# State-space recurrence taken in steps of two, and one half gate tile in four split by VectorE

## The chip, the cores and the metric

The kernel runs on one core of a Trainium2 chip. The metric is the device time of one execution in microseconds, lower is better. Engines: TensorE (PE in the profile, its weight loads PEld), VectorE (DVE), ScalarE (ACT), GpSimd (POOL), SyncE (SP).

## What is computed

An encoder block on 256 tokens of width 2048 with 16 meta tokens put ahead (272 positions): a projection `h @ w_in` gives the state-space inputs, queries, keys, values and 32 tiles of gates. A bidirectional state-space mixer and a windowed attention run in parallel, are gated, merged and projected, and a product-key expert network follows. The part that the change rewrites:

```python
a = exp(lam * dt)                        # complex, per group and state
bu = einsum('lgc,gpc->lgp', u, Bbar)     # 16 channels -> 64 states
h[l] = a * h[l-1] + bu[l]                # forward, and once more backward
y = real(einsum('lgp,gcp->lgc', h, C))
y = gelu(y_fwd + y_bwd + d_skip * u)
...
gates = h_norm @ w_in[:, gates] + b_gate # 32 tiles of 128 columns
```

## The kernel before

Products that want fp32 precision are made from a high part (`float32r`) and a low part of each operand, three matmuls in place of one: high by high, high by low, low by high.

The stage that the change touches runs two loops in step with each other, in 32 steps and a few to drain. **The gate tiles**: gate tile n (16 blocks of 128 by 128 weights, contracted with 256 tokens) comes in two halves, h = 2n and 2n+1; half h lies in slot q = h mod 4 of `halves`, the high part in `gate_hi(q)`, the low in `gate_lo(q)`. For every half GpSimd's queue issues two transfers. `cast_half(h)` (L385) loads the weights into `gate_hi` with the cast to `float32r`. ScalarE writes the negative of it into `gate_lo` (`minus_high`, L523), and `rest_half(h)` (L389) loads the same weights again and adds them there, so that weights minus high part remain. The order on the queue is cast(h+1), rest(h), cast(h+2), rest(h+1), and each waits in line: an even cast for the first half of the tile before it to be used by TensorE (`s_gh`), an odd cast for tile h//2 - 2 to be finished (`s_wdone`), a rest for its `minus_high`. TensorE multiplies the half in `half_gate` (L1269 to L1271, 24 matmuls of 256 columns), two steps behind (`LAG`).

**The recurrence**: in step t (four steps to a column tile of 128 channels, `cc`) the four engines handle two groups of states in one direction. ScalarE makes turning angles, sines and cosines over 272 positions (L516, L517, L541 to L544). TensorE projects the inputs to states (`state_inputs`, L1312, 12 matmuls into four banks of `ps`). VectorE turns them back by the angle (L910, L911, L916, L917), so that the complex recurrence becomes two real ones, scans them (L926, four scans of 272), turns forward again (L937, L938) and takes real parts (L945). TensorE multiplies by the output matrices (`state_outputs`, L1326), which ScalarE and VectorE build (L533, L890, L891). VectorE adds the direct term (`take_y`, L952).

The order of the work is written out by hand. VectorE's step t begins with the products of tile t-2 (L910), then real parts of t-3, the scans, the angles and L937, L938. TensorE's step t is: first half of gate tile t-2, `state_inputs` of t-1, which waits for VectorE's products of t-2 because both use the same banks, `state_outputs` of t-3, second half of gate tile t-2. Every engine takes its instructions in order.

Of the kernel before, what the change touches and what calls it, by code (L numbers as in the profile page):

```python
# [56 lines left out]
NSC = 6  # L57


def build(nc, W, keys, par, bw, cw, meta, x, gffn, gfin, u_tab, v_tab, out):  # L60
    top = ExitStack()
    with top:
# [48 lines left out]
        scur = sbt(mix, "scur", [P, 2, NSC, SPC])  # L111
# [10 lines left out]
        bwH = sbt(scan, "bwH", [P, 2, 2, 2, P], F32R)  # L122
        cp = sbt(scan, "cp", [P, 2, 2, SPC, 32])
        cs = sbt(scan, "cs", [P, 4, SPC, 32])
        tb = sbt(scan, "tb", [P, 2, 2, L])
        ang = sbt(scan, "ang", [P, 2, 2, L])
        trig = sbt(scan, "trig", [P, 2, 2, 2, L])
        pa = sbt(scan, "pa", [P, 2, 2, L])
        pb = sbt(scan, "pb", [P, 2, 2, L])
# [3 lines left out]
        gated = sbt(post, "gated", [P, 2, 2, SEQ])  # L133
# [7 lines left out]
        def in_hs2(at):  # L141
            return h2f[:, at * D:(at + 1) * D].rearrange("p (s u r t) -> p s u r t", s=2, u=2, r=2)
        oc, os_ = in_hs2(0), in_hs2(1)

# [93 lines left out]
        s_cp = sem("s_cp")  # L238
        s_bu = sem("s_bu")
# [13 lines left out]
        s_gh = sem("s_gh")  # L253
        s_gel, s_sgg, s_glu, s_sig, s_ya = sem("s_gel"), sem("s_sgg"), sem("s_glu"), sem("s_sig"), sem("s_ya")
# [43 lines left out]

        def gate_hi(q):
            return halves[:, q, :]  # L300

        def gate_lo(q):
            return halves[:, 4 + q, :]

# [10 lines left out]
        def _(sp):  # L315
# [15 lines left out]
            with sp.Fori(0, CT // 2) as b:  # L331
                for cc in range(2):
                    sp.wait_ge(s_bu, PPC * (2 * b + cc) + PPC)
                    sp.dma_start(bwt[:, cc, :, :, :].rearrange("p d r s -> p (d r s)"),
                                 bw[bass.ds(2 * b + cc, 1), :, :].rearrange("a p n -> (a p) n")).then_inc(s_bw[cc], 16)
                    sp.wait_ge(s_cp, 2 * (2 * b + cc) + 2)
                    sp.dma_start(cwt[:, cc, :, :, :].rearrange("p i r c -> p (i r c)"),
                                 cw[bass.ds(2 * b + cc, 1), :, :].rearrange("a p n -> (a p) n")).then_inc(s_cw[cc], 16)
# [21 lines left out]
        def _(pool):  # L360
# [63 lines left out]
        def _(act):  # L424
# [81 lines left out]
            def turns(b, t):  # L506
# [7 lines left out]
                for u in range(2):  # L514
                    turn = scur[:, cc, 0, at + 2 * u:at + 2 * u + 1]
                    nc.scalar.activation(tb[:, t % 2, u, :], iota, ACT.Copy, scale=turn)  # L516
                    ins = nc.scalar.activation(ang[:, t % 2, u, :], iota, ACT.Identity, scale=turn, bias=magic[:, :])  # L517
                ins.then_inc(s_tb, 1)

            def minus_high(b, t, half):  # L520
                use, q = gate_half(b, t, half)
                act.wait_ge(s_gc[q], 16 * use + 16)
                nc.scalar.activation(gate_lo(q), gate_hi(q), ACT.Copy, scale=-1.0).then_inc(s_gn, 1)  # L523

            def out_products(b, cc, k):

                ct = 2 * b + cc
                if k == 0:
                    act.wait_ge(s_cw[cc], 16 * b + 16)
                    act.wait_ge(s_cp, 2 * ct + 4)  # L530
                c, co = ((0, 2), (1, 3), (0, 4), (1, 2))[k]
                for i in range(SPC):
                    ins = nc.scalar.activation(cs[:, k, i, :], cwt[:, cc, i, c, :], ACT.Copy, scale=scur[:, cc, co, i:i + 1])  # L533
                ins.then_inc(s_cpl, 1)
# [19 lines left out]
            def inputs_high(b, cc):  # L554
                nc.scalar.activation(uP[:, cc, 0, :], ucur[:, cc, :], ACT.Copy).then_inc(s_inH, 1)
                act.wait_ge(s_bw[cc], 16 * b + 16)
                nc.scalar.activation(bwH[:, cc, :, :, :].rearrange("p d r s -> p (d r s)"),
                                     bwt[:, cc, :, :, :].rearrange("p d r s -> p (d r s)"), ACT.Copy).then_inc(s_inH, 1)

            def scan_body(b, first=False):  # L560
                for t in range(PPL):
                    turns(b, t)
# [7 lines left out]
                    if t % PPC < 2:  # L570
                        for k in range(2):
                            out_products(b, t // PPC, 2 * (t % PPC) + k)
                    if t >= LAG + 1 or not first:
                        gate(*behind(b, t, LAG + 1))

            scan_body(0, first=True)
            with act.Fori(1, BODIES) as b:
                scan_body(b)
            minus_high(*behind(BODIES, 0, 1), 0)
# [4 lines left out]

            act.wait_ge(s_ye, 2 + CT)
# [119 lines left out]
        def _(dve):  # L705
            dve.sem_inc(s_cp, 4)
# [27 lines left out]
            def discretise():  # L734
# [48 lines left out]
                for k, a in enumerate((4, 10, 16, 18, 19)):  # L783
# [85 lines left out]
            def scalars(b, cc):  # L869
# [4 lines left out]
                                      scal[:, bass.ds(ct, 1), :, :].rearrange("p a k i -> p (a k i)")).then_inc(s_scur, 1)  # L874
                nc.vector.tensor_copy(ucur[:, cc, :], flat(ukT[:, bass.ds(ct, 1), :])).then_inc(s_scur, 1)
                dve.wait_ge(s_scur, 2 * ct + 2)

            def inputs_low(b, cc):
                dve.wait_ge(s_inH, 2 * (2 * b + cc) + 2)
                nc.vector.tensor_tensor(uP[:, cc, 1, :], ucur[:, cc, :], uP[:, cc, 0, :], ALU.subtract).then_inc(s_inL, 1)  # L880
                nc.vector.tensor_tensor(bwL[:, cc, :, :, :].rearrange("p d r s -> p (d r s)"),
                                        bwt[:, cc, :, :, :].rearrange("p d r s -> p (d r s)"),
                                        bwH[:, cc, :, :, :].rearrange("p d r s -> p (d r s)"), ALU.subtract).then_inc(s_inL, 1)

            def out_matrices(b, cc):

                ct = 2 * b + cc
                dve.wait_ge(s_cpl, 4 * ct + 4)
                dve.wait_ge(s_y, PPC * ct + PPC)
                nc.vector.tensor_tensor(cp[:, cc, 0], cs[:, 0], cs[:, 1], ALU.subtract).then_inc(s_cp, 1)  # L890
                nc.vector.tensor_tensor(cp[:, cc, 1], cs[:, 2], cs[:, 3], ALU.subtract).then_inc(s_cp, 1)  # L891
# [9 lines left out]
            def input_products(b, t):  # L901
# [4 lines left out]
                bu = ps[:, 2:6, 0:L].rearrange("p (u r) t -> p u r t", u=2)  # L906

                def turn(k):
                    return trig[:, s, k, :, :].rearrange("p u (o t) -> p u o t", o=1).broadcast_to([P, 2, 2, L])
# [9 lines left out]
            def scans(b, t):  # L919
                n, cc = PPL * b + t, t // PPC  # L920
                at = units(t).start
                for k in range(2):
                    dve.wait_ge(s_gin, 2 * n + 1 + k)
                    for u in range(2):
                        r = scur[:, cc, 1, at + 2 * u:at + 2 * u + 1].broadcast_to([P, L])
# [3 lines left out]
            def turned_back(b, t):  # L929

                s, n, kept = t % 2, PPL * b + t, slice(0, SEQ) if t % 2 else slice(META, L)
# [3 lines left out]
                def turn(k):  # L935
                    return trig[:, s, k, :, kept].rearrange("p u (o t) -> p u o t", o=1).broadcast_to([P, 2, 2, SEQ])
                nc.vector.tensor_tensor(oc[:, s], turn(0), pa[:, :, :, kept], ALU.mult).then_inc(s_oc, 1)  # L937
                nc.vector.tensor_tensor(os_[:, s], turn(1), pa[:, :, :, kept], ALU.mult).then_inc(s_os, 1)  # L938
# [9 lines left out]
            def take_y(b, cc):  # L948

                ct = 2 * b + cc  # L950
                dve.wait_ge(s_y, PPC * ct + PPC + PPL)
                nc.vector.scalar_tensor_tensor(flat(yT[:, bass.ds(ct, 1), :]), ucur[:, cc, META:L],  # L952
                                               scur[:, cc, 5, 0:1], ps[:, 6 + cc, 0:SEQ], ALU.mult, ALU.add
                                               ).then_inc(s_ye, 1)
# [11 lines left out]
            def scan_body(b, first=False):  # L966
                for t in range(PPL):
                    if t % PPC == 0:
                        scalars(b, t // PPC)
                        if first and t == 0:  # L970
                            angles(b, t)
                            inputs_low(b, 0)
                    pair(b, t, first)
                    if t == PPL - 1:
                        take_y(b, 0)
                    if t == PPC - 1 and not first:
                        take_y(b - 1, 1)
# [4 lines left out]
                    if t % PPC == 0 and not (first and t == 0):  # L982
                        inputs_low(b, t // PPC)
                    if t % PPC == 2:
                        out_matrices(b, t // PPC)

            scan_body(0, first=True)
            with dve.Fori(1, BODIES) as b:
                scan_body(b)
            for t in range(2):  # L990
                pair(BODIES, t)
                turned_back(*behind(BODIES, t, 2))
            real_parts(*behind(BODIES, 2, 3))
            take_y(BODIES - 1, 1)


# [153 lines left out]
        def _(pe):  # L1150
# [4 lines left out]
            pe.sem_inc(s_gh, 2)  # L1155

# [104 lines left out]
            def half_gate(b, t, half):  # L1261
# [3 lines left out]
                pe.wait_ge(s_ga[q], 16 * use + 16)  # L1265
# [31 lines left out]

            def state_inputs(b, t):
                n = PPL * b + t
                cc, way, jp = place(t)  # L1300
                if t % PPC == 0:
                    pe.wait_ge(s_inL, 2 * (2 * b + cc) + 2)
                pe.wait_ge(s_ab, 2 * n + 2)
                for r in range(2):
                    for part in range(3):
                        for u in range(2):
                            rows = slice(32 * (2 * jp + u), 32 * (2 * jp + u) + 32)
                            w = (bwL if part == 2 else bwH)[rows, cc, way, r, :]
                            x = uP[rows, cc, part % 2, :]
                            if way:  # L1310
                                x = x[:, L - 1::-1]
# [251 lines left out]
```

## Time and profile before

| | us |
|---|---|
| median of 3 runs (lowest, highest) | 2129.09 (2126.37, 2129.18) |
| profiled execution, its own time | 2125.94 |
| its span | 2124.1 |

| engine | busy us | share of the span |
|---|---|---|
| TensorE matmuls | 1744.0 | 82% |
| VectorE | 1381.1 | 65% |
| ScalarE | 549.3 | 26% |
| GpSimd | 804.1 | 38% |

The span falls into stages: projections and attention to about 205 us, the stage described above from there to 549 us (its last result is the GELU on `yT`), gating, merge and output projection to about 770 us, then the experts to the end. In the stage of the change GpSimd's instructions are few and short: most of its time is waiting. Times are microseconds, and those marked ns are nanoseconds.

### The profile page before, as it was taken

The numbers are of one execution on the slowest core, as the hardware profiler recorded it, in microseconds if no ns is written. First come the engines' busy times: TensorE is split into PE (matmuls) and PEld (weight loads), VectorE is DVE, ScalarE is ACT, GpSimd is POOL, SyncE is SP. The second block draws the span as 40 slices with busy tenths as digits, with TensorE's granted clock in tenths as the row PEclk, the third lists the DMA queues.
The fourth block names the chain that finished last, engine by engine and source line by source line (L and its number), as shares of the span: only waits on it lengthen the run. The fifth ranks groups of instructions, "written<-read, shape, count | busy, mean of one in ns | idle before, by whom it ended". The sixth has DMA issues, their size and how long they took to land.

```text
span 2124.1 us, 23420 instructions
## 1 busy us (share of the span) xinstructions
PE 1744.0 (82%) x7552; PEld 1078.5 (51%) x7552; DVE 1381.1 (65%) x2230; ACT 549.3 (26%) x1167; POOL 804.1 (38%) x686
## 2 busy tenths in 40 slices
PE   7987788888899998978977997777877777777776
PEld 6976677777799885524533543222322222222222
DVE  5444999999545446566565666666666666666654
ACT  5333877777434321010110110001001001000001
POOL 1041222222054014453544454543545654644431
PEclk9998899999999999999999999999999999999999
DMA  4430899999655569999999999999999999999997
GB/s 193 159 120 21 207 213 220 218 213 217 212 178 183 180 227 423 421 421 409 423 420 395 400 404 422 421 421 422 406 422 421 422 422 422 422 422 421 421 421 299
DMA packets 106665, 694.82 MB, mean 327 GB/s; under 512 B 11856, under 2 KB 11856, under 8 KB 30928
## 3 DMA queue, kind: packets, MB, share of 16 engines
q0 software_dynamic: 92160, 604.02, 74.9%
q1 hardware_dynamic: 14432, 89.90, 11.5%
q8 instruction: 36, 0.59, 0.1%
q14 instruction: 37, 0.30, 0.0%
HBM read 691.78 MB, written 2.10 MB: 327 GB/s over the span
## 4 chain that ended last, share of the span: by engine, by line
PE 37%; DMA 36%; DVE 10%; issue 9%; ACT 4%; POOL 3%; DVEq 0%; POOLq 0%; ACTq 0%; SPq 0%
DMA uv<-u_tab,eid 30%; PE ps L1466 14%; DMA halves<-W 6%; PE ps L1172 3%; PE ps L1416 3%; PE ps L1174 3%; PE ps L1173 3%; POOL uv L420 2%; DVE uv L1111 2%; PE ps L1399 1%; PE ps L1400 1%; PE ps L1398 1%; PE ps L1165 1%; ACT cs L533 1%; POOL uv L417 1%
## 5 line engine op out<-in xcount | busy, mean ns | idle before, releaser
L1466 PE MATMUL ps<-uv,dg 128*128 128x512 f32 x2048 | 953.7, 611 | 273.2 <-DVE dg L1117 267.8
L1111 DVE CUSTOM_DVE_ANT_0 uv<-uv,xn 128x2048 f32<-128x2048 f32 x256 | 587.1, 2293 | 378.2 <-DMA uv<-u_tab,eid 359.6
L1466 PEld LDWEIGHTS ps<-uv,dg 128*128 128x128 f32 x2048 | 378.2, 193 | 826.1 <-issue 462.2
L420 POOL DMA_INDIRECT uv<-v_tab,eid x256 | 273.1, 1067 | 601.8 <-PE ps L1466 347.8
L417 POOL DMA_INDIRECT uv<-u_tab,eid x256 | 344.5, 1346 | 199.8 <-issue 186.1
L678 ACT ACTIVATE ga<-av 128x1 f32<-128x1 f32 x256 | 51.9, 203 | 1180.9 <-DVE av L1111 1180.9
L1269 PE MATMUL ps<-hH,halves 128*128 128x256 f32 x512 | 154.4, 302 | 53.6 <-DMA halves<-W 31.7
L731 DVE TENSOR_TENSOR low_ring<-ring,wh 128x2048 fp32r<-128x2048 f32 x43 | 101.2, 2356 | 76.4 <-ACT wh L440 76.3
L1270 PE MATMUL ps<-hLx,halves 128*128 128x256 f32 x512 | 148.4, 290 | 0.0
L1271 PE MATMUL ps<-hH,halves 128*128 128x256 f32 x512 | 148.2, 289 | 0.0
L389 POOL DMA_DIRECT2D halves<-W x64 | 55.7, 870 | 222.6 <-ACT halves L523 222.6
L1269 PEld LDWEIGHTS ps<-hH,halves 128*128 128x128 f32 x512 | 101.3, 198 | 71.9 <-issue 34.1
L1117 DVE TENSOR_SCALAR dg<-prm,ga,gw 128x128 f32<-128x128 f32 x256 | 93.7, 366 | 67.6 <-ACT ga L678 32.3
L440 ACT ACTIVATE wh<-ring 128x2048 fp32r<-128x2048 f32 x52 | 99.5, 1914 | 137.3 <-PE ps L1174 98.1
L1270 PEld LDWEIGHTS ps<-hLx,halves 128*128 128x128 f32 x512 | 101.5, 198 | 0.0
L1271 PEld LDWEIGHTS ps<-hH,halves 128*128 128x128 f32 x512 | 101.3, 198 | 0.0
L1416 PE MATMUL ps<-h2T,ring 128*128 128x256 f32 x448 | 100.8, 379 | 0.0
L1416 PEld LDWEIGHTS ps<-h2T,ring 128*128 128x128 f32 x448 | 85.1, 190 | 21.7 <-issue 11.5
L1172 PE MATMUL ps<-hH,wh 128*128 128x272 f32 (+1 forms) x288 | 85.6, 297 | 2.0 <-DVE hL L816 1.1
L523 ACT ACTIVATE halves<-halves 128x1024 fp32r<-128x1024 f32 x64 | 67.6, 1056 | 68.8 <-DMA halves<-W 68.7
L1173 PE MATMUL ps<-hL,wh 128*128 128x272 f32 (+1 forms) x288 | 82.9, 288 | 0.0
L1174 PE MATMUL ps<-hH,low_ring 128*128 128x272 f32 (+1 forms) x288 | 82.8, 288 | 0.0
(247 smaller groups left out, 2359.4 us busy)
## 6 DMA issues: line engine op xcount, KB each, us to landing
ring<-W SPq DMA_DIRECT2D x72, 1024.0 KB, 4.8
halves<-W POOLq DMA_DIRECT2D x128, 512.0 KB, 6.8
xn<-x SPq DMA_DIRECT2D x4, 1024.0 KB, 9.8
uv<-u_tab,eid POOLq DMA_INDIRECT x256, 15.3
uv<-v_tab,eid POOLq DMA_INDIRECT x256, 14.0
bwt<-bw SPq DMA_DIRECT2D x8, 256.0 KB, 7.2
cwt<-cw SPq DMA_DIRECT2D x8, 256.0 KB, 7.2
out<-xn SPq DMA_DIRECT2D x4, 512.0 KB, 5.5
```

What stands on the lines that cost most here:

```text
L417: pool.indirect_dma_start(uv[:, s, 0, :], None, u_tab, at).then_inc(s_u[s], 16)
L420: pool.indirect_dma_start(uv[:, s, 1, :], None, v_tab, at).then_inc(s_vv[s], 16)
L731: nc.vector.tensor_tensor(low_ring[:, n % RING, :], ring[:, n % RING, :], high_slot(n), ALU.subtract).then_inc(s_low, 1)
L1111: nc.vector.tensor_tensor_reduce(uv[:, j % UV, 0, :], uv[:, j % UV, 0, :], xn[:, T, :], 1.0, 0.0, ALU.mult, ALU.add, av[:, hh, j:j + 1]).t ...
L1172: nc.tensor.matmul(dst, wh[:, block0 + k, :], xh(k), start=(k == 0), stop=False)
L1173: nc.tensor.matmul(dst, wh[:, block0 + k, :], xl(k), start=False, stop=False)
L1174: ins = nc.tensor.matmul(dst, wl[:, block0 + k, :], xh(k), start=False, stop=(k == last))
L1269: nc.tensor.matmul(ps[:, t % 2, 0:SEQ], wh[:, m, :], hH[:, k, META:L], start=(k == 0), stop=False)
L1270: nc.tensor.matmul(ps[:, t % 2, 0:SEQ], wh[:, m, :], hLx[:, k, :], start=False, stop=False)
L1271: ins = nc.tensor.matmul(ps[:, t % 2, 0:SEQ], wl[:, m, :], hH[:, k, META:L], start=False, stop=(k == KT - 1))
L1416: ins = nc.tensor.matmul(ps[:, 4 + q % 2, 0:SEQ], w[:, k, :], h2T[:, k, :], start=(k == 0), stop=(k == KT - 1))
L1466: ins = nc.tensor.matmul(ps[:, 4 * T + n, :], dg[:, j % 2, :], uv[:, j % UV, 1, n * 512:(n + 1) * 512], start=False, stop=last and i == 2 ...
```

## The change

The recurrence goes in steps of two: `h[l+1] = a*a*h[l-1] + (a*Bbar*u[l] + Bbar*u[l+1])`. The scan then runs over 136 elements, and so do angles, sines and turning products. The projection to states now takes even and odd positions with two sets of weights, `Bbar` and `a*Bbar`; the second is built per column tile by a transpose on TensorE (`input_turns`), a copy on ScalarE (`input_rows`), six VectorE products and sums (`stepped_inputs`) and a transpose back (`stepped_turns`). Outputs at the positions in between come from output matrices multiplied by `a`, so these have 64 columns, and from a direct term `kb` (TensorE `direct_terms`, 16 small matmuls for each column tile, and VectorE `direct_terms`), which also takes in `d_skip`. Output products move from ScalarE to VectorE, and `take_y` from VectorE to ScalarE. Ten small VectorE steps join the discretisation.

Of the gate halves, those with q = 3 (each second half of an odd tile) are loaded plainly into `plain`, a part of the weight ring free in this stage. VectorE subtracts the high part (`gate_rest`, once in every even step), for which it waits for both transfers; the plain load is queued where the accumulating one was, after `cast_half(h+1)`, and waits for nothing itself. `minus_high` is left out for these.

```diff
+        plain = ring[:, RING - 1, D // 2:D]
             def rest_half(h):
-                pool.wait_ge(s_gn, h + 1)
-                pool.dma_start(gate_lo(h % 4), half_weights(h), accum_op=ALU.add).then_inc(s_ga[h % 4], 16)
+                if h % 4 == 3:
+                    pool.dma_start(plain, half_weights(h)).then_inc(s_ga[3], 16)
+                else:
+                    pool.wait_ge(s_gn, 3 * (h // 4) + h % 4 + 1)
+                    pool.dma_start(gate_lo(h % 4), half_weights(h), accum_op=ALU.add).then_inc(s_ga[h % 4], 16)
...
+            def input_rows(b, cc):
+                act.wait_ge(s_bt, ct + 1)
+                act.wait_ge(s_kb, ct + 1)
+                nc.scalar.activation(bs[cc]..., ps[:, 4, :], ACT.Copy).then_inc(s_bs, 1)
+            def take_y(b, cc):
+                for j in range(4):
+                    for q in range(2):
+                        ins = nc.scalar.activation(..., ACT.Copy)
...
+            def stepped_inputs(b, cc):
+                nc.vector.tensor_copy(acur..., scal...).then_inc(s_acur, 1)
+                for k, (r, c) in enumerate(((0, 0), (1, 1), (1, 0), (0, 1))):
+                    nc.vector.tensor_tensor(am[:, k], bs[cc]..., four(acur[:, c, :]), ALU.mult).then_inc(s_am, 1)
+                for r, op in enumerate((ALU.subtract, ALU.add)):
+                    nc.vector.tensor_tensor(ab[:, :, r, :]..., am[:, 2 * r], am[:, 2 * r + 1], op).then_inc(s_abm, 1)
...
+            def out_products(b, cc, q):
+                for k, (c, of) in enumerate(((cre, kr), (cim, ki), (cre, kn), (cim, kr))):
+                    nc.vector.tensor_tensor(cs[:, k], c, co(of), ALU.mult).then_inc(s_cpl, 1)
...
+            def gate_rest(b, t):
+                use, q = gate_half(b, t, 1)
+                dve.wait_ge(s_gc[q], 16 * use + 16)
+                dve.wait_ge(s_ga[q], 16 * use + 16)
+                nc.vector.tensor_tensor(gate_lo(q), plain, gate_hi(q), ALU.subtract).then_inc(s_glo, 1)
...
                     pair(b, t, first)
                     if not (first and t == 0):
                         angles(b, t)
                     if t >= 2 or not first:
                         turned_back(*behind(b, t, 2))
+                    if t % 2 == 0 and (t or not first):
+                        gate_rest(*behind(b, t, 1))
+                    if t % PPC == 0:
+                        if not (first and t == 0):
+                            inputs_low(b, cc)
+                        out_products(b, cc, 0)
+                    elif t % PPC == 1:
+                        out_matrices(b, cc, 0)
+                        out_products(b, cc, 1)
+                    elif t % PPC == 2:
+                        out_matrices(b, cc, 1)
+                        if not (last and cc):
+                            stepped_inputs(*after(b, t))
+                    else:
+                        direct_terms(b, cc)
...
             def half_gate(b, t, half):
-                pe.wait_ge(s_ga[q], 16 * use + 16)
+                if q == 3:
+                    pe.wait_ge(s_glo, use + 1)
+                else:
+                    pe.wait_ge(s_ga[q], 16 * use + 16)
...
             def state_inputs(b, t):
                 for r in range(2):
+                    for odd in range(2):
+                        for part in range(3):
+                            for u in range(2):
+                                ins = nc.tensor.matmul(ps[:, 2 + u, r * H2:(r + 1) * H2], w, x, ...)
...
                     if t >= 1 or not first:
                         state_inputs(*behind(b, t, 1))
+                    if t % PPC == 1 and not (last and cc):
+                        input_turns(*after(b, t))
+                    if t % PPC == 3:
+                        direct_terms(b, cc, last and cc == 1)
+                        if not (last and cc):
+                            stepped_turns(*after(b, t))
                     if t >= 3 or not first:
                         state_outputs(*behind(b, t, 3))
```

## Rows read from the trace of the kernel before

**Rows 1.** Windows; window, length, busy by engine (instructions), granted clock, DMA share, GB/s.

```profile
291.00:332.00 41.00, 35.72 (x292) 30.47 (x290) 40.60 (x55) 30.73 (x71) 11.34 (x16) 0.96 0.96 223
```

**Rows 2.** Timeline of VectorE, one step; start, duration, line, operation, shapes.

```profile
329.88 0.43 DVE L880 TENSOR_TENSOR uP<-ucur,uP 128x272 fp32r<-128x272 f32 x1
330.24 0.68 DVE L881 TENSOR_TENSOR bwL<-bwt,bwH 128x512 fp32r<-128x512 f32 x1
330.84 1.28 DVE L910 TENSOR_TENSOR pa<-ps,trig 128x1088 f32<-128x1088 f32 x1
...
333.24 0.68 DVE L945 TENSOR_TENSOR hs<-hs 128x512 f32<-128x512 f32 x1
333.84 0.72 DVE L916 TENSOR_TENSOR pa<-pa,pb 128x544 f32<-128x544 f32 x1
...
335.11 2.56 DVE L926 TENSOR_TENSOR_SCAN pa<-scur,pa 128x272 f32<-128x272 f32 x4
337.59 0.70 DVE L898 SCALAR_TENSOR_TENSOR ang<-ang,tb 128x544 f32<-128x544 f32 x1
338.20 1.22 DVE L937 TENSOR_TENSOR hs<-trig,pa 128x1024 f32<-128x1024 f32 x1
339.34 1.22 DVE L938 TENSOR_TENSOR hs<-trig,pa 128x1024 f32<-128x1024 f32 x1
340.67 1.29 DVE L910 TENSOR_TENSOR pa<-ps,trig 128x1088 f32<-128x1088 f32 x1
```

**Rows 3.** Timeline, issues of half tiles and those who waited for their landing.

```profile
356.83 0.86 POOL L389 DMA_DIRECT2D halves<-W  x1 [3.27 <-ACT halves L523]
357.38 0.87 POOL L385 DMA_DIRECT2D halves<-W  x1
360.60 0.88 POOL L389 DMA_DIRECT2D halves<-W  x1 [2.35 <-ACT halves L523]
361.41 0.62 POOL L385 DMA_DIRECT2D halves<-W  x1
...
363.12 0.58 PE L1269 MATMUL ps<-hH,halves 128*128 128x256 f32 x1 [2.00 <-DMA halves<-W]
364.39 1.06 ACT L523 ACTIVATE halves<-halves 128x1024 fp32r<-128x1024 f32 x1 [0.84 <-DMA halves<-W]
...
367.47 0.28 PE L1271 MATMUL ps<-hH,halves 128*128 128x256 f32 x1
...
368.05 0.55 POOL L385 DMA_DIRECT2D halves<-W  x1 [1.43 <-PE ps L1271]
...
368.69 1.06 ACT L523 ACTIVATE halves<-halves 128x1024 fp32r<-128x1024 f32 x1 [0.67 <-DMA halves<-W]
```

**Rows 4.** From issue to landing, of the casting loads (L385, 64 of them).

```profile
DMA to landing us min/median/max: 3.9/7.0/9.0
```

**Rows 5.** From issue to landing, of the accumulating loads (L389, 64 of them).

```profile
DMA to landing us min/median/max: 5.2/6.8/9.3
```

**Rows 6.** Timeline of TensorE, inputs, outputs and a second half's start.

```profile
355.46 0.52 PE L1312 MATMUL ps<-uP,bwH 32*128 32x272 f32 x4
...
356.41 1.49 PE L1326 MATMUL ps<-hs,cp 128*32 128x256 f32 x12
...
358.02 0.39 PE L1269 MATMUL ps<-hH,halves 128*128 128x256 f32 x1
```

**Rows 7.** Windows around a wait of TensorE's; columns as in rows 1.

```profile
361.00:363.20 2.20, 0.20 (x2) 0.09 (x1) 1.85 (x5) 1.60 (x4) 1.03 (x2) 0.99 1.02 302
363.20:366.50 3.30, 3.30 (x16) 3.30 (x17) 3.30 (x5) 2.46 (x5) 0.76 (x1) 0.50 0.92 194
...
342.00:344.00 2.00, 0.00 (x0) 0.00 (x0) 2.00 (x3) 2.00 (x10) 0.55 (x1) 1.00 1.06 268
344.00:346.00 2.00, 1.82 (x15) 1.82 (x16) 2.00 (x4) 2.00 (x5) 0.00 (x0) 1.00 1.00 231
```

**Rows 8.** Lines of the attention stage: transposes on TensorE.

```profile
L1247 PE MATMUL ps<-prm,pr 128*128 128x128 f32 x32 | 6.9, 301 | 0.0
```

More of the change, by code:

```diff
@@ L569, in scan_body @@
                         minus_high(*behind(b, t, 1), 1)
-                    if t % PPC < 2:
-                        for k in range(2):
-                            out_products(b, t // PPC, 2 * (t % PPC) + k)
+                    if t % PPC == 2 and not (last and t > PPC):
+                        input_rows(*after(b, t))
                     if t >= LAG + 1 or not first:
                         gate(*behind(b, t, LAG + 1))
+                    if t == PPL - 1:
+                        take_y(b, 0)
+                    if t == PPC - 1 and not first:
+                        take_y(b - 1, 1)
             scan_body(0, first=True)
-            with act.Fori(1, BODIES) as b:
+            with act.Fori(1, BODIES - 1) as b:
                 scan_body(b)
+            scan_body(BODIES - 1, last=True)
             minus_high(*behind(BODIES, 0, 1), 0)
@@ L964, in pair, with scan_body @@
                     scans(*behind(b, t, 2))
[L966 removed]
+            def scan_body(b, first=False, last=False):
                 for t in range(PPL):
+                    cc = t // PPC
                     if t % PPC == 0:
[L969 removed]
+                        scalars(b, cc)
                         if first and t == 0:
+                            stepped_inputs(b, 0)
                             angles(b, t)
@@ L981, in scan_body @@
                         turned_back(*behind(b, t, 2))
[L982 to L985, printed above, removed]
+                    if t % 2 == 0 and (t or not first):
[13 more added lines that the diff above has]
+                        direct_terms(b, cc)
+            dve.wait_ge(s_wdone, RING + W_GATE)
+            for j in range(4):
+                nc.vector.tensor_copy(eye32[32 * j:32 * j + 32, :], ident[32 * j:32 * j + 32, 32 * j:32 * j + 32]).then_inc(s_eye, 1)
+            for a in (oc, os_):
+                nc.vector.memset(a[:, 1, :, :, 0:1], 0.0).then_inc(s_eye, 1)
+            dve.wait_ge(s_eye, 6)
             scan_body(0, first=True)
-            with dve.Fori(1, BODIES) as b:
+            with dve.Fori(1, BODIES - 1) as b:
                 scan_body(b)
+            scan_body(BODIES - 1, last=True)
             for t in range(2):
@@ L992, in _ @@
                 turned_back(*behind(BODIES, t, 2))
+                if t == 0:
+                    gate_rest(*behind(BODIES, t, 1))
             real_parts(*behind(BODIES, 2, 3))
-            take_y(BODIES - 1, 1)
             dve.wait_ge(s_ybh, 1)
```

251 lines of the change are left out of this document (184 added, 67 removed).

## The prediction

> **What bounds the kernel now.** I read the page's row of busy tenths first, to find the stage, then the windows, then the timeline of one step, then who waits for whom. In a window of 41 us GpSimd issues 16 transfers, which is four gate tiles, so a tile takes 10.25 us and two tiles 20.5 us [rows 1]. VectorE is busy for 40.6 of the 41 us: it is the bound. The DMA engines are at 0.96 beside it, TensorE's matmuls at 35.7 of 41 and ScalarE at 30.7. VectorE's step is 9.83 us from one L910 to the next [rows 2]; once in four steps extras come on top. The reader is to see two things in the rows: VectorE is full, and it waits for no transfer. Everything that a half gate tile needs passes over DMA, ScalarE, GpSimd's queue and TensorE, in a ring that VectorE is not part of.
>
> **What the change takes off.** From the spacing of starts, an operation of 272 elements takes 0.36 us, one of 512 takes 0.60, of 544 some 0.62 and of 1024 1.14 [rows 2]; on that line 256 elements are 0.34 and 128 are 0.22. The step has two products at 1.20, real parts at 0.60, two sums at 0.63, four scans at 0.62, the angles at 0.61 and two products at 1.14: 9.8. With halved lengths that is 2 x 0.62 + 0.35 + 2 x 0.36 + 4 x 0.35 + 0.36 + 2 x 0.60 = 5.3 us.
>
> Added on VectorE: `gate_rest`, 1024 elements, 1.14 in each even step. In a step t mod 4 = 0 `inputs_low` (0.36 + 2 x 0.60) and `out_products` (4 x 0.34), 2.9 in all; in t mod 4 = 2 four matrix parts of 128 (0.9) and `stepped_inputs` (six of 256, a small copy, two waits, 2.3), 3.2 in all; the mean after `gate_rest` is k = 3.05. Odd steps get 2.3 or 0.2, 1.2 in the mean. Two steps: 2 x 5.3 + 1.14 + 3.05 + 1.2 + 0.2 (scalars) = 16.2, or 8.1 a tile in place of 10.25. If VectorE's work were all, the stage would gain 69 us over 32 tiles.
>
> DMA: of four transfers in flight, the ones issued at 356.83 and 357.38 land at 363.1 and 364.35, and the cast issued at 361.41 at 368.65, behind one more accumulating load [rows 3]. So a cast takes 1.3 us of the queue and a pair 4.3, which leaves 3.0 for an accumulating load. Two tiles now use about 19.5 us (20.5 x 0.96 [rows 1]); one accumulating load turned into a plain one, taken at a cast's price, saves 1.7: 17.8. (A plain load isn't in these rows; the ends are nothing, were it as slow as an accumulating one, and a cast's 1.3 or a little less.)
>
> TensorE, over two tiles: four half tiles at 2.85 (24 x 0.118 [rows 6]); inputs 24 matmuls of 136 columns in place of 12 of 272, which took 0.95 [rows 6]: between 0.95, were it columns that count, and 1.9, were it instructions; each still loads weights of 128 columns, so I take 1.6. Outputs took 1.42 to 1.6 and halve to 0.8. New: in t mod 4 = 1 four transposes (0.5, as these overlap [rows 8]), in t mod 4 = 3 four more and 16 fp32 matmuls of 32 columns, which by L1326's way of counting are 32 records. At 0.05 each that is 1.6; ends 1.0 and 3.8 (0.118 each, as with 256 columns [rows 6]). Mean over odd steps 1.3, ends 0.7 and 2.4. Direct terms in even steps 0.5. Sum 18, or 9 a tile. The Trainium skill's page "TensorE: Matmul & The Clock Gate" (section "Wait — 56ns, not 53.3ns?") puts the least spacing of matmuls at about 25 ns; by that figure, as an estimate, the 32 records would cost 0.8 and the sum below would be 6 us lower.
>
> So by work alone two tiles would take about 18 us and the gain would be 16 x 2.5 = 40 us. That isn't what I forecast.
>
> **The wait that the change adds.** `gate_rest(n)`, n odd, is in VectorE's queue in step n+1, and everything behind it waits with it: k, then step n+2, whose first operations are the products of tile n. For these TensorE's `state_inputs` of n+1 waits, and behind that in its queue are outputs and the second half of gate tile n; only after this second half may the next cast into slot 3 be issued. So there is now a ring through VectorE, once for two tiles. I follow it from E, the end of TensorE's step n:
> - The cast of half 2n+1 is issued at +0.3 (TensorE's last matmul of a half to GpSimd's issue is some 0.3: the L1271 that starts at 367.47 ends at 367.75, the issue is at 368.05 [rows 3]). The accumulating load of half 2n follows at +1.1, since its `minus_high` is long done. The cast of 2n+2 waits for TensorE's first half in step n+1: +3.3. Only then the plain load is issued: +3.85.
> - When does it land? By the extremes [rows 4, 5] it is 3.9 to 9.3 us after the issue, +7.75 to +13.1; the median of 7 would be +10.9. Queue work gives a value between: the first cast lands at the least at +4.2, then 3.0, 1.3 and 1.3: +9.8. I take +9.8, since the queue is empty at E in the new rhythm.
> - VectorE would get to `gate_rest` at about +5: it stands still for nearly 5 us. Then 0.05 + 1.14 + k 3.05 + products 1.24: +15.3.
> - TensorE has finished step n+1 at +8.7 and the first half in step n+2 at +11.65; it stands still for 3.6. Then inputs 1.6, extras 1.3, outputs 0.8, second half 2.85: +21.9.
>
> That is 21.9 for two tiles, where 20.5 stood.
>
> **TensorE's clock.** After a wait from 361 to 363.1, the clock is 0.50 (1.2 GHz in place of 2.4) for 3.3 us; 16 matmuls in 3.3 us, 0.21 each in place of 0.118, cost 1.5 us. After a wait of 2 us from 342 to 344 it stays at 1.00 [rows 7]. A standstill of 3.6 us on each round is longer than both. I take 1.2 of the 1.5: 23.1 for two tiles (ends 0 and 1.7). The page "TensorE: Matmul & The Clock Gate" of the Trainium skill (section "Part 1: The HAM clock gate") says that the slow clock is the default and that activity releases it: by that rule a longer idle stretch makes the fall surer, the sum would be 16 x 0.3 = 5 us higher, and without any fall 19 lower. The clock row after the wait agrees with it; the later wait without a fall leaves open from which length it holds.
>
> **Sum.** 16 rounds x (23.1 - 20.5) = 41.6. At the start, VectorE's extra chain (`stepped_inputs`, two transposes) is offset by the 3.5 us of output products that ScalarE no longer does: +1. At the end the drain is shorter by 5 and `take_y` longer by 2: -3. Ten small steps in the discretisation lie before attention, where VectorE waits for TensorE's first scores: nothing, and 3 if that cover were gone. Everything behind the stage is unchanged. Together +40 on the profiled execution's 2125.94 (span 2124.1 and 1.8 around it): 2166. The median of the runs shown is 3 us higher than that execution, which the range covers.
>
> **Rivals.**
> - *The ring holds, but fast* (faster). The plain load lands 3.9 us after its issue (+7.75), as the fastest cast did; inputs cost 0.95 and extras 0.7, and the clock stays up. Then 7.75 + 1.2 + 2.9 + 1.24 + 0.95 + 0.7 + 0.8 + 2.85 = 18.4, near the 18 of work: 16 x -2.1 - 2, about 2090. For it: the queue has less to do. Against it: three transfers are ahead of the plain one. With only some of it true the time lies between 2090 and 2126; the point at which it turns is a landing about 2.6 us earlier than I take, at +7.2, or the same sum from other terms.
> - *The slow ring*. The clock falls on each round, landing at the median of 7 (+10.9), small matmuls at the instruction's price (inputs 1.9, extras 2.4): 26.2 for two tiles, +91, minus 2: 2215.
> - *The plain load brings nothing to the queue*, being as slow as an accumulating one: landing 1.7 later, 16 x 1.7 more than the forecast: 2193.
>
> **How the numbers follow.** Forecast 0.55, fast ring 0.22, slow ring 0.13, plain load no faster 0.05, and 0.05 that terms cancel within 0.2% (about what a measurement of this kernel can tell from no change). Slower 0.73, same 0.06, faster 0.21. The range takes in half of the fast ring's stretch and most of the slow one's: 2105 to 2208.
>
> **What would show it.** In the changed kernel VectorE waits for DMA ahead of `gate_rest`, 16 times, 4 to 5 us each; its busy share in the stage falls from 0.99 to about 0.72; TensorE waits for VectorE's second product once in two steps, for 3 to 4 us, and its clock is at 0.5 after it. L910's duration is 0.70. The DMA share falls to about 0.8. The forecast is wrong if VectorE's waits at `gate_rest` are under 2 us, or if two tiles take under 20 us with the waits there: then landing or TensorE's tail is mis-sized.

## The result

The changed kernel takes 2238.72 us (median of 4 runs, 2237.09 to 2239.19) against 2129.14 before: a ratio of 1.0517, 95% interval 1.0504 to 1.053. It is 110 us slower, where 40 were forecast, above the range's end of 2208. Direction and mechanism came as forecast; the price was sized too low by more than half.

Most of the loss lies in the stage of the change. Its last result, the GELU on `yT`, begins at 648.16 us in place of 549.07, which is 99 of the 113 us between the two profiled spans. Another 4 us come between there and the experts' first gather, and 10 between the experts' first and last gather (the two times at the end of each line, before and after):

```profile
L417 POOL DMA_INDIRECT uv<-u_tab,eid x256: 944/948/3051, 788.8 to 2092.4; - x128
L441 POOL DMA_INDIRECT uv<-u_tab,eid x256: 943/949/3058, 892.3 to 2206.3; - x128
```

The change doesn't touch the experts. In the profiles of all fourteen kernels here that last stretch takes either 1303 to 1305 us or 1314 to 1316, and what decides isn't known; the kernel of experiment 3, whose profile has the longer one, spreads over 11.5 us from run to run. So a difference of some 10 us between two totals is read below together with the start of the first gather.

Windows of the changed kernel (columns as in [rows 1]):

```profile
300.00:400.00 100.00, 77.29 (x707) 70.35 (x706) 54.67 (x136) 38.72 (x87) 20.64 (x31) 0.84 0.67 166
400.00:500.00 100.00, 78.81 (x737) 71.28 (x737) 60.87 (x149) 40.28 (x95) 19.55 (x29) 0.80 0.64 157
```

Against [rows 1], VectorE falls from 40.6 of 41 us to 55 to 61 of 100, DMA from 0.96 to 0.66, TensorE's clock from 0.96 to 0.82. No engine is full: the stage waits for itself. Where, is told by the answer on the subtraction's line (L1064), "idle before it until" with us and times:

```profile
L1064 DVE TENSOR_TENSOR halves<-ring,halves x16: 1224/1226/1226, 233.3 to 636.3; 128x1024 fp32r<-128x1024 f32 x16
  DMA ring<-W: 175.6, 16
```

VectorE stands 11 us before each of the 16 subtractions. One round in the timelines, first GpSimd's issues (L406 casts, L413 accumulating loads, L410 the plain one):

```profile
385.34 0.55 POOL L406 DMA_DIRECT2D halves<-W  x1 [11.08 <-PE ps L1402]
385.87 0.92 POOL L413 DMA_DIRECT2D halves<-W  x1
388.17 0.55 POOL L406 DMA_DIRECT2D halves<-W  x1 [1.38 <-PE ps L1402]
388.70 0.55 POOL L410 DMA_DIRECT2D ring<-W  x1
...
412.34 0.55 POOL L406 DMA_DIRECT2D halves<-W  x1 [11.45 <-PE ps L1402]
```

then VectorE:

```profile
396.66 1.23 DVE L1064 TENSOR_TENSOR halves<-ring,halves 128x1024 fp32r<-128x1024 f32 x1 [9.14 <-DMA ring<-W]
397.80 0.89 DVE L992 TENSOR_TENSOR cp<-cs 128x128 f32<-128x128 f32 x4
...
400.95 0.71 DVE L1021 TENSOR_TENSOR pa<-ps,trig 128x544 f32<-128x544 f32 x1
401.58 0.71 DVE L1022 TENSOR_TENSOR pb<-ps,trig 128x544 f32<-128x544 f32 x1
```

and TensorE:

```profile
396.68 0.28 PE L1402 MATMUL ps<-hH,halves 128*128 128x256 f32 x1
402.35 0.69 PE L1484 MATMUL ps<-uP,bwH 32*128 32x136 f32 x4 [5.39 <-DVE pb L1022]
```

The ring closes in 27.0 us, from cast to cast. TensorE frees slot 3 at 385.03 (0.3 before the cast); the plain load is issued at +3.7 and the subtraction starts at +11.6; the products are done and TensorE resumes at +17.3; its tail of inputs, extras, outputs and second half takes 9.7. Over ten rounds (the plain loads seen in the chain from 252.10 to 525.09) the mean is 27.3, in place of 20.5 [rows 1]. At both ends of the stage the rounds are shorter: over the whole stage TensorE's gate tiles take 99.6 us more, 6.2 for each of the 16 rounds (before, and changed):

```profile
L1269 PE MATMUL ps<-hH,halves x512: 274/281/583, 220.1 to 543.6; 128*128 128x256 f32 x171
L1400 PE MATMUL ps<-hH,halves x512: 274/281/582, 219.5 to 642.6; 128*128 128x256 f32 x171
```

One thing to add on the change: `plain` and `gate_lo(3)` are the same bytes, since `halves` shares its memory with the weight ring, so the subtraction is in place.

### The profile page after: what moved, and what is told of

It is laid out like the page before. It is cut to its first block, busy times and chain, and to the rows that moved or that the text cites. A ratio compares the mean times of both kernels' runs of the same rounds, so it can differ in the third digit from the quotient of the medians.

```text
span 2237.3 us, 25162 instructions
## 1 busy us (share of the span) xinstructions
PE 1818.0 (81%) x8384; PEld 1156.8 (52%) x8384; DVE 1312.2 (59%) x2443; ACT 470.9 (21%) x975; POOL 811.0 (36%) x686
## 4 chain that ended last, share of the span: by engine, by line
PE 41%; DMA 34%; issue 9%; DVE 9%; POOL 4%; ACT 1%; DVEq 0%; POOLq 0%; SPq 0%; ACTq 0%
DMA uv<-u_tab,eid 27%; PE ps L1660 13%; DMA ring<-W 6%; PE ps L1610 3%; PE ps L1301 3%; PE ps L1300 3%; PE ps L1302 3%; POOL uv L444 2%; PE ps L1484 2%; DVE uv L1238 2%; PE ps L1400 2%; POOL uv L441 2%; PE ps L1401 1%; PE ps L1402 1%; PE ps L1293 1%
## 5 line engine op out<-in xcount | busy, mean ns | idle before, releaser
L1660 PE MATMUL ps<-uv,dg 128*128 128x512 f32 x2048 | 964.0, 617 | 272.5 <-DVE dg L1244 261.8
L441 POOL DMA_INDIRECT uv<-u_tab,eid x256 | 357.9, 1398 | 204.5 <-DVE eid L1218 109.9
L1484 PE MATMUL ps<-uP,bwH 32*128 32x136 f32 x512 | 66.9, 359 | 90.5 <-DVE pb L1022 88.1
L406 POOL DMA_DIRECT2D halves<-W x64 | 39.7, 620 | 267.8 <-PE ps L1402 245.8
L1064 DVE TENSOR_TENSOR halves<-ring,halves 128x1024 fp32r<-128x1024 f32 x16 | 19.6, 1225 | 175.6 <-DMA ring<-W 175.6
L1484 PEld LDWEIGHTS ps<-uP,bwH 32*128 32x128 f32 x512 | 55.0, 259 | 96.0 <-DVE pb L1022 71.4
L1610 PEld LDWEIGHTS ps<-h2T,ring 128*128 128x128 f32 x448 | 85.0, 190 | 21.8 <-issue 11.5
```

Source lines behind the costliest of these rows:

```text
L441: pool.indirect_dma_start(uv[:, s, 0, :], None, u_tab, at).then_inc(s_u[s], 16)
L1484: ins = nc.tensor.matmul(ps[:, 2 + u, r * H2:(r + 1) * H2], w, x, start=(odd == 0 and part == 0), stop=(odd == 1 and part == 2))
L1610: ins = nc.tensor.matmul(ps[:, 4 + q % 2, 0:SEQ], w[:, k, :], h2T[:, k, :], start=(k == 0), stop=(k == KT - 1))
L1660: ins = nc.tensor.matmul(ps[:, 4 * T + n, :], dg[:, j % 2, :], uv[:, j % UV, 1, n * 512:(n + 1) * 512], start=False, stop=last and i == 2 ...
```

## The experiments

The theory (R): the ring through VectorE's wait costs the time. The rivals: (W) the halved recurrence itself is dear, with more and smaller instructions; and, on the size, that the late landing or TensorE's long tail has another cause than the one named for it.

### 1. Recurrence in steps of two alone

```diff
-                if h % 4 == 3:
-                    pool.dma_start(plain, half_weights(h)).then_inc(s_ga[3], 16)
-                else:
+                pool.wait_ge(s_gn, h + 1)
+                pool.dma_start(gate_lo(h % 4), half_weights(h), accum_op=ALU.add).then_inc(s_ga[h % 4], 16)
...
-                    if t % 2 == 0 and (t or not first):
-                        gate_rest(*behind(b, t, 1))
```

> The changed kernel with the fourth half loaded as before: cast, negative on ScalarE, accumulating load; VectorE takes no part in it. Theory R (the ring over VectorE's wait for two transfers, landing 11.6 us after TensorE frees the slot, costs the 110 us): the ring is gone, two tiles go back from 27.3 us to 19.5 to 20.5 (the DMA engines' 19.5 us of work is the next bound), the time is 2105 to 2130, and VectorE waits for no transfer. Theory W (the halved recurrence itself is dear: more and smaller matmuls and VectorE operations, more hand-overs between engines): most of the slowdown stays, above 2190.

Measured: 2125.62 us, ratio 0.9986 (0.997 to 1.0001). All of the slowdown is gone, so theory W falls (the first gather starts at 789.8 us, before at 788.8, changed at 892.3). But the recurrence in twos brings nothing either:

```profile
291.00:332.00 41.00, 38.04 (x377) 34.19 (x375) 29.05 (x77) 23.64 (x52) 11.17 (x16) 0.92 0.95 217
```

VectorE has come down from 40.6 us to 29 [rows 1], and a tile still takes 10.25 us (16 issues in 41 us): the DMA engines are at 0.95. Experiments 5 and 6 test that reading.

### 2. Plain load and subtraction alone

The kernel before with `plain`, `gate_rest` and its waits at the places of the change.

```diff
+                if h % 4 == 3:
+                    pool.dma_start(plain, half_weights(h)).then_inc(s_ga[3], 16)
...
                         turned_back(*behind(b, t, 2))
+                    if t % 2 == 0 and (t or not first):
+                        gate_rest(*behind(b, t, 1))
```

> The kernel before with only the plain load and VectorE's subtraction put in at the same places, the recurrence in steps of one. Theory R: VectorE is full and still has to wait, so two tiles are landing 12.2 + subtraction 1.2 + low parts or matrices 0.8 + products 2.4 + inputs 1.1 + outputs 1.6 + second half 3.4 = 22.7 us in place of 20.5: 16 x 2.2 = 35 us slower, 2150 to 2180. Rival (only the subtraction's own time counts, VectorE being the bound): 16 x 1.14 = 18 us slower, 2147. Theory W: no more than that 18, since the recurrence is as before.

Measured: 2198.51 us, ratio 1.0333 (1.0303 to 1.0363): 70 us slower, above the expected range, twice what R gave and four times the subtraction's own time. So the wait does the harm, on either recurrence. With its own longer step, VectorE arrives later and waits less (53.2 us in all, 3.3 each), but VectorE was full before and has no slack to give; the clock falls here too:

```profile
332.00:373.00 41.00, 28.55 (x208) 22.74 (x208) 33.78 (x45) 25.65 (x64) 7.68 (x11) 0.83 0.71 174
```

The ring is shown by this run; my 22.7 us for its length was 2 us short (20.5 + 70/16 = 24.9), and no run takes that apart.

### 3. The subtraction moved off the ring

```diff
                     real_parts(*behind(b, t, 3))
+                if t % 2 and (t >= 3 or not first):
+                    gate_rest(*behind(b, t, 2))
...
-                    if t % 2 == 0 and (t or not first):
-                        gate_rest(*behind(b, t, 1))
```

> The changed kernel with the subtraction moved behind the products and real parts of the next odd step, the loads in their places. Theory R: the landing is no longer ahead of the products for which TensorE waits; VectorE doesn't wait for a transfer any more, two tiles are bounded by the work of TensorE and DMA, 18 to 19.5 us, time 2085 to 2115. Theory W: above 2210, VectorE's waits only change their place.

Measured: 2117.01 us, ratio 0.9946 (0.9929 to 0.9964). The same loads, the same subtractions, the same work, with the subtraction behind the products in VectorE's order instead of ahead of them: 122 us faster than the changed kernel and 11 faster than the one before. The first gather starts at 778.9 us, 10 earlier than before. It misses R's range of 2085 to 2115 by 2 us, and R was wrong that VectorE would wait for no transfer. The waits still sum to 49.4 us, but they are no longer ahead of the products:

```profile
387.69 1.23 DVE L1064 TENSOR_TENSOR halves<-ring,halves 128x1024 fp32r<-128x1024 f32 x1 [0.40 <-DMA ring<-W]
409.25 1.23 DVE L1064 TENSOR_TENSOR halves<-ring,halves 128x1024 fp32r<-128x1024 f32 x1 [4.12 <-DMA ring<-W]
```

### 4. The terms of the ring, one by one

**k, the work behind the subtraction.** It goes to the end of the even step:

```diff
                     else:
                         direct_terms(b, cc)
+                    if t % 2 == 0 and (t or not first):
+                        gate_rest(*behind(b, t, 1))
```

> The changed kernel with the subtraction moved to the end of its even step, behind low parts, output products, matrix parts and stepped inputs (3.05 us in the mean), loads in their places. Theory R: these 3 us come off the ring, VectorE's wait shrinks from 11 to 8 us, two tiles take 24.2 us, 16 x 3.05 = 49 less: 2180 to 2200. If the clock recovers with the shorter idle time, up to 20 less than that. Theory W (work, not order): no change, 2230 to 2245.

Measured: 2191.7 us, ratio 1.0282 (1.0251 to 1.0312), 47 less than the changed kernel where 49 were expected. VectorE's waits sum to 127.3 us, 8.0 each, in place of 11. Only the order on one engine has changed, and the time follows what lies between landing and products.

**The clock.** 44 matmuls of 256 columns fill TensorE's idle time. (They add products of `hH` into columns that nobody reads.)

```diff
+                    if t % 2 and gated_now:
+                        for i in range(44):
+                            nc.tensor.matmul(ps[:, t % 2, SEQ:2 * SEQ], hH[:, 1, META:META + P], hH[:, 0, META:L],
+                                             start=False, stop=False, skip_group_check=True)
                     if t >= 1 or not first:
                         state_inputs(*behind(b, t, 1))
```

> The changed kernel with 44 matmuls of 256 columns added on TensorE in each odd step between the first half of the gate tile and the state inputs, where it stands idle for 5.4 to 7 us; they add hH products into unused columns, which nobody reads. 44 x 0.118 = 5.2 us fit into the idle time. Theory C (3.3 us of each ring of 27.3 us are TensorE's slow clock after its idle time): the clock stays at 1.00, the 24 input matmuls take 1.65 in place of 2.83 us, the ring is 24 us, the time falls by 16 x 3.3 = 53 to 2175 to 2195, with more work done. Rival (small matmuls cost 0.118 each at any clock): unchanged, 2235 to 2250.

Measured: 2199.64 us, ratio 1.0333 (1.031 to 1.0355), 39 us less than the changed kernel, with more work done; that is short of the 53 that were expected and outside the range, and far from the rival's "unchanged". A window of this kernel:

```profile
300.00:400.00 100.00, 93.94 (x956) 86.91 (x955) 64.07 (x158) 43.58 (x100) 21.56 (x32) 0.98 0.75 183
```

Against 0.84 in the same window of the changed kernel the clock is nearly whole. In the chains of the two, the 24 input matmuls (L1484) take 2.83 us in the changed kernel and 1.73 in the filled one:

```profile
402.35 2.83 PE ps L1484 x24
```

```profile
311.23 1.73 PE ps L1484 x22
```

The landing is nearly as it was (median 8.2 us after the issue, 8.4 in the changed kernel). So filling gives back 39 of the 110 us, 2.4 a round, by the clock. That isn't all that the clock costs, since the filled kernel doesn't keep it in every round. In the round whose inputs start at 311.23 TensorE had still stood idle for 1.6 us, and the clock fell during the work behind it:

```profile
314.00:316.00 2.00, 2.00 (x14) 1.66 (x11) 1.97 (x7) 1.38 (x4) 0.00 (x0) 0.50 0.50 98
```

**The transfers ahead of the plain load.** The accumulating load between the two casts is cut to 128 of its 1024 columns, which leaves the low part of these halves incomplete.

```diff
+                    n = P if h % 4 == 2 else D // 2
-                    pool.dma_start(gate_lo(h % 4), half_weights(h), accum_op=ALU.add).then_inc(s_ga[h % 4], 16)
+                    pool.dma_start(gate_lo(h % 4)[:, 0:n], half_weights(h)[:, 0:n], accum_op=ALU.add).then_inc(s_ga[h % 4], 16)
```

> The changed kernel with the accumulating load of the first half of each odd tile (the one issued between the two casts, ahead of the plain load) cut to 128 of 1024 columns; the low part of these halves is left incomplete. If the transfers ahead in the queue set the plain load's landing (8.4 us after issue in the changed kernel), it comes down by 2.6 to 3.2 to some 5.5 us, and the ring of 27.3 by as much: 16 x 2.9 = 46 less, 2180 to 2205. If the landing is its own latency, nothing changes: 2230 or more.

Measured: 2189.55 us, ratio 1.0285 (1.0268 to 1.0302), 49 us less, as expected. From issue to landing of the plain load, in the changed kernel and in this one:

```profile
DMA to landing us min/median/max: 7.4/8.4/9.4
```

```profile
DMA to landing us min/median/max: 5.3/5.5/6.7
```

The 2.9 us that the landing loses are the 49 us over 16 rounds (3.1 each).

**The place of the issue.** The plain load goes ahead of the next cast, behind the accumulating load:

```diff
             for h in range(2 * GATES):
                 if h + 1 < 2 * GATES:
                     cast_half(h + 1)
-                rest_half(h)
+                if h % 4 != 3:
+                    rest_half(h)
+                if h % 4 == 2:
+                    rest_half(h + 1)
```

> The changed kernel with the plain load issued right behind the accumulating load of the half before it, ahead of the next cast, instead of behind it. Ring theory: issue at +1.4 in place of +3.65 us, and one cast less ahead in the queue, so the landing is 3.3 us earlier: 24 us for two tiles, 16 x 3.3 = 53 less: 2175 to 2200. If only issue order behind the accumulating load mattered (no cast's share), 36 less: 2203.

Measured: 2206.52 us, ratio 1.0363 (1.0345 to 1.038), 32 less: 2 us a round. That misses the range of 2175 to 2200 and is near the smaller of the two expected values, 2203: the issue comes 2.3 us earlier in the round, and the landing takes as long behind it as before (median 8.5 us), so one cast less ahead in the queue brought nothing on top.

The plain load right behind its own cast, ahead of the accumulating load as well:

```diff
                     cast_half(h + 1)
+                    if (h + 1) % 4 == 3:
+                        rest_half(h + 1)
-                rest_half(h)
+                if h % 4 != 3:
+                    rest_half(h)
```

> The changed kernel with one thing moved: the plain load is issued right behind the cast of the same half, ahead of the accumulating load and of the next cast. Theory R: it lands some 6.5 us after TensorE frees the slot in place of 11.6, VectorE waits 1 to 2 us in place of 11 at each subtraction, two tiles take 18.5 to 20 us, the time is 2085 to 2120. Theory W: under 20 us of the 110 come back, above 2210. If the transfers' work and not their order sets the landing, both loads still end after the accumulating one and VectorE waits 6 us or more.

Measured: 2136.35 us, ratio 1.0029 (1.0012 to 1.0047). 102 of the 110 us come back by moving one issue, but it isn't the 2085 to 2120 of theory R. The landing took 6.8 us (median), issued at +0.8, so VectorE still waits 68.0 us in all, 4.3 each; and a new wait has come, TensorE's first half for the accumulating load that is now behind:

```profile
328.13 0.36 PE L1403 MATMUL ps<-hH,halves 128*128 128x256 f32 x1 [3.94 <-DMA halves<-W]
```

These gains (47, 39, 49, 32 and 102 us) can't be added up: whatever shortens the wait also shortens TensorE's idle time, and with it what the low clock costs.

### 5. What the recurrence alone could bring

The recurrence in twos with all accumulating loads cut to 128 columns (low parts incomplete):

```diff
-                pool.dma_start(gate_lo(h % 4), half_weights(h), accum_op=ALU.add).then_inc(s_ga[h % 4], 16)
+                pool.dma_start(gate_lo(h % 4)[:, 0:P], half_weights(h)[:, 0:P], accum_op=ALU.add).then_inc(s_ga[h % 4], 16)
```

> Recurrence in steps of two, all four halves by accumulating loads as before, but each of these loads cut to 128 of 1024 columns (low parts incomplete). Theory: with full loads the DMA engines (0.95 busy) took VectorE's place as the bound and the recurrence alone brought nothing. With short loads two tiles fall to TensorE's 18 us or a little more: 2075 to 2105. Rival (hand-overs between engines hold the step at 10.2 us): 2120 or more.

Measured: 2086.88 us, ratio 0.9804 (0.9788 to 0.982).

```profile
291.00:332.00 41.00, 41.00 (x454) 37.22 (x453) 32.65 (x88) 26.09 (x58) 12.77 (x18) 1.00 0.61 155
```

TensorE is now busy for all of the 41 us. The time lies within the expected 2075 to 2105.

### 6. The kernel before with the same cut

> The kernel before with the same cut of all accumulating loads. Theory: VectorE's 9.83 us step plus extras bounds it whatever the transfers do: 2118 to 2129, at most 10 us gained at the stage's start. Rival (DMA bounds it as well): 2100 or less.

Measured: 2126.15 us, ratio 0.9987 (0.9977 to 0.9996).

```profile
291.00:332.00 41.00, 36.03 (x286) 30.57 (x285) 40.60 (x55) 30.95 (x74) 11.44 (x16) 0.92 0.49 129
```

With DMA at 0.49 in place of 0.96 it gains 3 us: VectorE bounded the kernel before, and the transfers did not. Against this run, the recurrence of experiment 5 with the same short loads gains 39 us. So the recurrence's gain was there, and in experiment 1 the transfers held it back: at 0.96 beside a full VectorE before, they took its place as the bound at almost the same pace.

### 7. Two more versions

Early load and late subtraction together:

> Plain load issued right behind its cast and subtraction moved behind the products and real parts of the next odd step, both. By the ring theory the late subtraction already takes the landing off the ring (2117), and the early load only puts the accumulating load 1 to 2 us later, for which TensorE's first half waits: no gain over the late subtraction alone, 2112 to 2125. If the landing still counted there, it would be 2105 or less.

Measured: 2136.34 us, ratio 1.0052 (1.003 to 1.0074), slower than the late subtraction alone and outside what I expected. VectorE's waits for the plain load are down to 7.2 us; what remains is as in the early load alone, the accumulating load that arrives later: from 250 to 480 us TensorE waits 16.8 us for it, with the late subtraction alone 6.9. That this is the whole of it was not tested. In its profile the first gather starts at 784.5 us, 4 earlier than before, and the experts take the longer of their two times, so the stage itself isn't shown to be slower than before.

Late subtraction, and both second halves (two in four) loaded plainly and split by VectorE:

```diff
+                if h % 2:
+                    pool.dma_start(plain[h % 4 // 2], half_weights(h)).then_inc(s_ga[h % 4], 16)
...
+                if t >= 2 or not first:
+                    gate_rest(*behind(b, t, 2))
```

> Late subtraction, and both second halves (two halves in four) loaded plainly and split by VectorE. Another accumulating load becomes plain in two tiles (1.7 us of DMA work), ScalarE loses 1.06, VectorE gains 1.14 and has room. Ring theory: no landing ahead of the products; bounded by TensorE's 18 us of work in two tiles and DMA's 16: 2090 to 2115. Rival: the landing of the plain loads, issued behind two others, makes TensorE wait for the subtraction in its second half: 2115 or more.

Measured: 2110.06 us, ratio 0.9916 (0.9894 to 0.9938), the lowest median of the full kernels: 19 us under the one before and 129 under the changed one. The first gather starts at 768.3 us, 20 earlier than before and 11 earlier than in experiment 3.

```profile
373.00:414.00 41.00, 39.13 (x416) 35.71 (x415) 36.70 (x88) 20.71 (x50) 10.57 (x17) 1.00 0.87 242
```

DMA is at 0.87, VectorE at 36.7 and TensorE at 39 of 41 us: some of what VectorE gained by the recurrence is spent where DMA was short.

## Why the prediction was right and wrong

- **The bound before** was VectorE: right, shown by experiment 6 and [rows 1].
- **The wait that the change adds, and the ring it closes**: right, shown from three sides: without the plain load no slowdown (1), the plain load alone slow (2), the same work with the subtraction behind the products faster than before (3). Of the signs, TensorE's wait for the second product and the clock at 0.5 behind it came as named; the waits at the subtraction were 11 us in place of 4 to 5, VectorE's share 0.58 in place of 0.72 and DMA's 0.66 in place of 0.8, all as in a longer ring.
- **VectorE's new work**: right. Subtraction and k take 4.3 us in the round shown and the way to TensorE's resumption 1.4, together 5.7 against 5.5 forecast; taking k off the ring gave 47 us for 49.
- **The landing**: too small. I took 5.95 us after the issue; the median was 8.4, and 8.0 in the round shown. The step that failed is the queue work by which I priced it, "+4.2, then 3.0, 1.3 and 1.3", and the reason given for it, that the queue is empty at E. It is empty, but that doesn't make it quick. From the freeing of the slot the four transfers of the round shown landed at +4.8, +8.7, +10.2 and +11.6 (4.5, 7.9, 7.1 and 7.9 us behind their issues). The last two steps, a cast and the plain load, were near right with 1.5 and 1.3; the first cast took 0.6 more, and the accumulating load behind it 3.9 in place of 3.0, the price that I had from a full queue [rows 3]. These are the transfers' rates from the empty queue on:

```profile
384.00:386.00 2.00, 2.00 (x19) 2.00 (x19) 2.00 (x7) 0.78 (x3) 0.66 (x2) 1.00 0.00 0
386.00:388.00 2.00, 2.00 (x20) 1.87 (x19) 1.51 (x3) 1.07 (x3) 0.79 (x1) 1.00 0.78 215
388.00:390.00 2.00, 2.00 (x33) 1.68 (x34) 0.00 (x0) 0.00 (x0) 1.08 (x2) 1.00 0.72 115
390.00:392.00 2.00, 2.00 (x26) 1.62 (x21) 0.00 (x0) 0.00 (x0) 0.00 (x0) 1.00 0.92 172
392.00:394.00 2.00, 1.99 (x18) 1.81 (x17) 0.00 (x0) 0.00 (x0) 0.00 (x0) 1.00 0.98 285
```

  The low rates, 115 and 172 GB/s from 388 to 392, fall where the first cast ends (it lands at 389.8) and the accumulating load is next (it lands at 393.8). That it is this load which is slow by itself is only argued from these rows; that it costs the plain load 2.9 us is shown by the run with it cut. The median of [rows 4, 5], which I had and set aside, would have given 1.1 of the 2.4 us that were missing. The rival in which a plain load is as slow as an accumulating one falls: it landed 1.3 us behind the cast ahead of it.
- **TensorE's tail**: too small, by the clock. I gave it 6.55 us and 1.2 for the clock, 7.75; it took 9.7. At full clock the sum was right: in the filled kernel the tail that starts at 336.27 takes 6.5, with 1.73 for the inputs (1.6 taken) and less for the extras (the 32 records of the direct terms 0.40, 1.6 taken). The term that failed is the clock's: the low clock costs some 3.2 us of this tail, not 1.2, since it lasts longer than in [rows 7]:

```profile
396.90:402.30 5.40, 0.06 (x1) 0.00 (x0) 5.33 (x15) 4.03 (x12) 2.08 (x3) 0.75 0.89 194
402.30:409.60 7.30, 7.25 (x78) 6.40 (x79) 6.89 (x19) 2.49 (x6) 0.00 (x0) 0.50 0.48 102
409.60:412.00 2.40, 2.40 (x22) 2.40 (x21) 2.40 (x8) 2.38 (x6) 0.00 (x0) 0.95 0.00 0
```

  In [rows 7] it was 3.3 us of dense work at 0.50; here it is 7.3 us after the resumption. The Trainium skill's page "TensorE: Matmul & The Clock Gate" (section "Part 1: The HAM clock gate") has activity as what releases the clock; that agrees with the filled kernel's 0.98. I had priced one such stretch, of dense matmuls; here the idle time is longer (5.4 us, since the landing was late too) and ends in small matmuls. Which of the two makes the clock stay low for 7.3 us of work wasn't tested.
- **Sum**: with 11.6 to 12.1 for the landing, 5.7 to the products and 9.7, the ring is 27.0 to 27.5 in place of 23.1; 16 x 4.2 = 67 on top of 2166 is 2233, and 2239 were measured. Part of that closeness is luck: the stage as a whole lost 99 us where 40 were forecast, 59 more, since the rounds at its ends are shorter than 27.3, and the 14 us behind the stage, which I had put at nothing, make up the rest. My slow ring (2215, chance 0.13; its terms add up to 26.0 us, not 26.2) had both terms, but as separate mishaps. They hang together, since a later landing makes TensorE's idle time longer.
- **By work alone the change would gain 40 us**: wrong in the kernel as it was asked. Experiment 1 gives 3 us, which is no more than its interval, and experiment 3 gives 11. The 18 us of TensorE for two tiles came out when the transfers were cut (experiment 5: 42 us gained, 39 against experiment 6). The 17.8 of DMA rest on 20.5 x 0.96 taken as 19.5, which is 19.7; in experiment 3 the DMA engines are at 0.91 and TensorE is busy for 157 of 164 us from 250 to 414 us, both nearly full, and two tiles take 19.3 us (from the first subtraction at 232.7 to the last at 522.1).

## What to carry to other kernels

Before a wait for a transfer is put on an engine, follow its queue behind the wait to whoever frees the slot for the next transfer: if it comes back to the same transfer, the landing time, the work queued behind the wait and the other engine's tail add up and are the new period, however idle all engines are. Here the kernel with the subtraction ahead of the products was 110 us slower than before, and the one with it behind them 11 faster. Size such a ring with the transfers in flight that it will have, and count the idle time that it gives TensorE as lost clock too.

## What the runs showed of the hardware

An accumulating load of 512 KB took about 3.0 us of a full queue (an estimate from the landings of [rows 3]). In a queue that started empty it landed 3.9 us behind the cast ahead of it, and cutting it to an eighth took 2.9 us off the landing of the plain load (8.4 to 5.5), at a DMA share of only 0.66. TensorE's clock stayed at 0.50 for 7.3 us of work after 5.4 us of idle time, and 44 useless matmuls in that idle time (5.2 us of work, an estimate from 0.118 each) made the kernel 39 us faster.
